# Forgetting attention with two products instead of three: high and low halves side by side in the array

## The reference

```
proj = u @ w_in                      # q, k, v, g (1024 columns each), fl (16 columns)
c = cumsum(log_sigmoid(fl + b_f))    # one value per row and head
for each head (16, of 64 columns), each block of 128 query rows:
    s = (qb @ k.T) * 0.125 + (cb[:, None] - c[None, :])      # causal, else -inf
    out = softmax(s) @ v
y = (out * silu(g)) @ w_out
```

## Time and profile before

| | |
|---|---|
| median of 3 runs | 3930.71 us (3926.98 to 3938.69) |
| profiled execution | 3930.58 us, span 3928.6 us |
| TensorE busy | 3640.7 us (93%) |
| VectorE busy | 2038.1 us (52%) |
| ScalarE busy | 1672.7 us (43%) |
| POOL busy | 108.0 us (3%) |
| mean granted TensorE clock | 0.951 |

### The profile page before, as it was taken

One profiled execution on the slowest core, in us unless ns is written; L12 is line 12 of the kernel. 1 busy time (PEld: TensorE's weight loads), 2 busy tenths in 40 slices (PEclk: granted clock), 3 DMA queues, 4 the chain that ended last, 5 costly groups with the idle time before them and its releaser, 6 DMA issues. The chain is left out here.

```text
span 3928.6 us, 48656 instructions
## 1 busy us (share of the span) xinstructions
PE 3640.7 (93%) x19058; PEld 2996.8 (76%) x19058; DVE 2038.1 (52%) x3959; ACT 1672.7 (43%) x3118; POOL 108.0 (3%) x119
## 2 busy tenths in 40 slices
PE   7999889999997999899897999999869999999799
PEld 6888558778876777777786877777758888888687
DVE  3144443453345677776335455555555456666552
ACT  3222561454442344443225444444443466665431
POOL 0011220000000000000000000000000000000000
PEclk9999999999997788989999999999979999999899
DMA  4343412113222211222311101010032121110321
GB/s 143 115 134 105 141 40 89 58 68 108 95 74 82 57 44 44 56 53 65 134 38 63 28 28 33 28 28 28 27 108 81 54 65 38 44 38 17 121 78 43
DMA packets 219339, 264.59 MB, mean 67 GB/s; under 512 B 62700, under 2 KB 142692, under 8 KB 218088
## 3 DMA queue, kind: packets, MB, share of 16 engines
q1 hardware_dynamic: 219112, 261.48, 20.6%
HBM read 191.43 MB, written 69.99 MB: 67 GB/s over the span
## 5 line engine op out<-in xcount | busy, mean ns | idle before, releaser
L332 PE MATMUL bank<-wh,XH 128*128 128x512 f32 x1344 | 536.3, 399 | 24.1 <-DVE wl L316 19.0
L332 PE MATMUL bank<-wh,XL 128*128 128x512 f32 x1344 | 529.1, 394 | 0.0
L332 PE MATMUL bank<-wl,XH 128*128 128x512 f32 x1344 | 528.5, 393 | 0.0
L2633 PE MATMUL bank<-XH,wh 128*128 128x512 f32 x1040 | 426.0, 410 | 28.2 <-DVE wl L2622 26.7
L2633 PE MATMUL bank<-XH,wl 128*128 128x512 f32 x1040 | 410.5, 395 | 0.0
L2633 PE MATMUL bank<-XL,wh 128*128 128x512 f32 x1040 | 409.6, 394 | 0.0
L332 PEld LDWEIGHTS bank<-wh,XH 128*128 128x128 f32 x1344 | 256.5, 191 | 77.9 <-DVE wl L316 12.6
L332 PEld LDWEIGHTS bank<-wl,XH 128*128 128x128 f32 x1344 | 255.8, 190 | 54.1
L332 PEld LDWEIGHTS bank<-wh,XL 128*128 128x128 f32 x1344 | 256.4, 191 | 51.0
L332 PE MATMUL bank<-XH,wh 128*128 128x512 f32 x704 | 280.8, 399 | 8.0 <-DVE XL L1585 8.0
L316 DVE TENSOR_TENSOR wl<-raw,wh 128x1024 fp32r<-128x1024 f32 x128 | 157.1, 1237 | 250.8 <-ACT wh L307 249.3
(11 more groups left out here) (419 smaller groups left out, 7155.0 us busy)
## 6 DMA issues: line engine op xcount, KB each, us to landing
sc_zt<-stage SPq DMA_DIRECT2D x88, 256.0 KB, 2.0
raw<-in_att_w_in SPq DMA_DIRECT2D x33, 512.0 KB, 4.1
raw<-in_even_w_in SPq DMA_DIRECT2D x32, 512.0 KB, 4.9
raw<-in_odd_w_in SPq DMA_DIRECT2D x32, 512.0 KB, 4.5
raw<-in_rec_w_in SPq DMA_DIRECT2D x32, 512.0 KB, 4.0
sc_h<-H SPq DMA_DIRECT2D x24, 512.0 KB, 2.6
sc_z<-stage SPq DMA_DIRECT2D x40, 256.0 KB, 2.0
z<-sc_z SPq DMA_DIRECT2D x8, 1024.0 KB, 5.8
```

The costliest lines, as they stand in the source:

```text
L332: done = e.matmul(out, lhsT, rhs, start=k == 0 and j == 0, stop=k == NK - 1 and j == 2)
L2633: done = e.matmul(bank[:, :], x[:, k, :], y[:, k, ts], start=k == 0 and j == 0, stop=k == NK - 1 and j == 2)
```

## The change

1. **Two products for scores.** The 64 rows beside the head's are now used. `qq` holds qh in the head's rows and ql in the other ones; `kk` holds kh in both. One product qq·kk gives high·high and low·high. The second, qx·kx, has qh and kl in the head's rows and the bias rows in the other ones. ScalarE makes two copies for each `load` instead of one.
2. **Two products for weighted.** v lies as [high, low] of one head (low, high for the other), so that one stationary operand gives vh·W in the head's 64 result rows and vl·W in the other 64. It meets WH, then WL. The two row halves must now be added: the new event `rest` copies the other rows from bank 5 to SBUF (ScalarE, 64x256), and `ve_mixed` adds them (64x256) and applies the gate in a second instruction that waits for the first.
3. **Gate.** Tanh of half the input instead of Sigmoid; plus one and times 0.5 are folded into the VectorE instructions.
4. **Order.** Low is done for n-2, behind the transposes of the same step and behind the maximum and scaling; `rest` and `mixed` are for n-5, in even steps; weight splits are at s = 2, 6, 10 and 14. Two events for n = 127 end the list.
5. **POOL.** The low halves of the seven blocks that come back are computed by POOL; buffers and later stages wait for its flag `xrest`.
6. The start-up fill clears two tiles for each head slot instead of four.

```diff
 def fox_order():
...
-        order += [("low", n - 3, 0)] * at(3) + [("turned", n - 2)] * at(2) + [("exps", n)] * at(0)
-        order += [("low", n - 3, 1)] * at(3) + [("normed", n - 1)] * at(1)
+        order += [("rest", n - 5)] * (at(5) and n % 2 == 0) + [("turned", n - 2)] * at(2) + [("exps", n)] * at(0)
+        order += [("normed", n - 1)] * at(1) + [("low", n - 2, half) for half in range(2)] * at(2)
+        order += [("mixed", n - 5)] * (at(5) and n % 2 == 0)
...
-            long |= {3: ("split", i + 1), 7: ("split", i + 2), 11: ("split", i + 3), 14: ("split", i + 4),
-                     8: ("load", 2 * p, "rows"), 9: ("load", 2 * p, "q"), 10: ("load", 2 * p, "k")}
...
+            long |= {8: ("load", 2 * p, "rows"), 9: ("load", 2 * p, "q"), 10: ("load", 2 * p, "k")}
...
+        if p < 8 and s % 4 == 2 and number[p, "q"] + s // 4 + 1 < len(seq):
+            order.append(("split", number[p, "q"] + s // 4 + 1))
...
+    order += [("rest", 127), ("mixed", 127)]
...
-            for j, (u, v) in enumerate((("qh", "kh"), ("ql", "kh"), ("qh", "kl"))):
+            for j, (u, v) in enumerate((("qq", "kk"), ("qx", "kx"))):
...
-            for j, (v, w) in enumerate(((vh, self.WH), (vl, self.WH), (vh, self.WL))):
-                done = e.matmul(bank[:, off:256], v[:, ks], w[x][:, kb, off:256], start=kb == top and j == 0,
-                                stop=kb == 0 and j == 2, skip_group_check=True)
+            off = P if kb == top else 0
+            for j, w in enumerate((self.WH, self.WL)):
+                done = e.matmul(bank[:, off:256], v[:, kb, :], w[x][:, kb, off:256], start=kb == top and j == 0,
+                                stop=kb == 0 and j == 1, skip_group_check=True)
...
+                scale, x, src = 0.125 if name == "q" else 1.0, self.x[n % 2], self.raw[name][hr, :]
+                e.activation(x[2 * name][hr, :], src, ACT.Copy, scale=scale).then_inc(*self.high.up("own", n, name))
+                second = x["qx"][hr, :] if name == "q" else x["kk"][self.other_rows(n), :]
+                e.activation(second, src, ACT.Copy, scale=scale).then_inc(*self.high.up(n, name))
...
+            if what == "rest":
+                h, x = n // 8, n // 2 % 2
+                e.wait_ge(*self.weighted.at(n))
+                if n >= 4:
+                    e.wait_ge(*self.mixed.at(n - 4))
+                e.activation(self.rest[x][self.rows_of(h)[0], :], c.banks[5][self.other_rows(h), 0:256], ACT.Copy).then_inc(*self.lower.up(n))
...
-            e.activation(self.half(self.g[p % 2], half), bank[:, :], ACT.Sigmoid).then_inc(*self.copied.up(p, name, half))
+            e.activation(self.half(self.g[p % 2], half), bank[:, :], ACT.Tanh, scale=0.5).then_inc(*self.copied.up(p, name, half))
...
+        e.wait_ge(*self.lower.at(n))
+        e.tensor_tensor(rest, self.c.banks[5][hr, 0:256], rest, ALU.add).then_inc(*self.mixed.up("sum", n))
+        e.wait_ge(*self.mixed.at("sum", n))
...
-        e.tensor_tensor(g, self.c.banks[5][hr, 0:256], g, ALU.mult).then_inc(*self.mixed.up(n))
+        e.scalar_tensor_tensor(out=g, in0=rest, scalar=0.5, in1=g, op0=ALU.mult, op1=ALU.mult).then_inc(*self.mixed.up(n))
...
+        for p in range(7):
+            e.wait_ge(*self.xhigh.at(p, 1))
+            e.tensor_tensor(self.c.XL[:, p, :], self.back_row(p), f32(self.c.XH[:, p, :]), ALU.subtract).then_inc(*self.xrest.up(p))
```

More of the change, by code:

```diff
@@ L2638 @@
 FOX_FIRST = ((0, "f", 0), (0, "q", 0))
-SPLITS = ("qh", "ql", "kh", "kl")
+SPLITS = ("qq", "kk", "qx", "kx")
 def fox_order():
@@ L2707, in __init__ @@
         self.tile = c.early("pe")
-        self.xlow = c.flag("ve")
+        self.xlow, self.xrest = c.flag("ve"), c.flag("po")
         self.w = HeadWeights(c, [win[:, 3984:4112]] + [win[:, at[name] + p * P:at[name] + (p + 1) * P] for p, name in self.seq[1:]],
-                             2, self.tile, [(self.xlow, (p, 1)) for p in range(7)])
+                             2, self.tile, [(self.xrest, (p,)) for p in range(7)])
         self.neg, self.negr, self.idr = c.const("neg"), c.sb("negr", [P, P], R32), c.sb("idr", [P, P], R32)
@@ L2732, in __init__ @@
         self.scored, self.turned, self.vturned, self.weighted = (c.flag("pe") for _ in range(4))
-        self.copied, self.high, self.expd, self.whigh, self.vhigh, self.xhigh, self.biased, self.logged = (c.flag("ac") for _ in range(8))
+        self.copied, self.high, self.expd, self.whigh, self.vhigh, self.xhigh, self.biased, self.logged, self.lower = (
+            c.flag("ac") for _ in range(9))
         self.ready, self.zeroed, self.low, self.most, self.scale, self.wlow, self.vlow, self.gated, self.mixed, self.summed = (
@@ L2736, in __init__ @@
         self.ones = c.flag("po")
-        self.marks = [[(self.xlow, (7, 123 + 4 * (s // 4)))] for s in range(NS)]
-        self.ends = [(self.xlow, (7, 127)), (self.ones, ())]
+        self.marks = [[(self.xrest, (6,))] * (s == 0) + [(self.xlow, (7, 123 + 4 * (s // 4)))] for s in range(NS)]
+        self.ends = [(self.xlow, (7, 127)), (self.xrest, (6,)), (self.ones, ())]
     def of(self, n):
@@ L2752, in rows_of, with other_rows, v_bank, v_high @@
         return slice(64 * (h % 2), 64 * (h % 2) + 64), 64 * (1 - h % 2)
+    def other_rows(self, h):
+        return slice(64 * (1 - h % 2), 64 * (1 - h % 2) + 64)
+    def v_bank(self, p, half):
+        return self.c.banks[self.mms[p, "v'", half]][:, :].rearrange("p (k a e) -> p k a e", k=4, a=2)
+    def v_high(self, p, half):
+        return self.v[p % 2][:, 4 * half:4 * half + 4, 0:4:3, :]
+    def v_low(self, p, half):
+        return self.v[p % 2][:, 4 * half:4 * half + 4, 1:3, :]
     def half(self, t, half):
@@ L2789, in sp @@
                 self.sp_rows(e, n)
-            elif what == "weighted" and n % 16 == 15 and n < 112:
+            elif what == "mixed" and n % 16 == 15 and n < 112:
                 p = n // 16
@@ L2952, in ac @@
                 e.activation(c.XH[:, n, :], self.back_row(n), ACT.Copy).then_inc(*self.xhigh.up(n, 1))
-            if what == "weighted" and n >= 112 and n % 4 == 3:
+            if what == "rest":
[4 more added lines that the diff above has]
+                e.activation(self.rest[x][self.rows_of(h)[0], :], c.banks[5][self.other_rows(h), 0:256], ACT.Copy).then_inc(*self.lower.up(n))
+            if what == "mixed" and n >= 112 and n % 4 == 3:
                 hr, half = self.rows_of(n // 8)[0], n % 8 // 4
@@ L3000, in ve @@
                 e.wait_ge(*self.copied.at(n, "g", rest[1]))
-                e.tensor_tensor(g, c.banks[self.mms[n, "g", rest[1]]][:, :], g, ALU.mult).then_inc(*self.gated.up(n, rest[1]))
+                e.scalar_tensor_tensor(out=g, in0=g, scalar=1.0, in1=c.banks[self.mms[n, "g", rest[1]]][:, :], op0=ALU.add, op1=ALU.mult) \
+                    .then_inc(*self.gated.up(n, rest[1]))
             elif what == "sums":
@@ L3029, in ve @@
                                     f32(self.WH[x][:, kbs[0]:kbs[-1] + 1, qs]), ALU.subtract).then_inc(*self.wlow.up(n, g))
[L3030 to L3034, removed]
+            elif what == "mixed":
+                self.ve_mixed(e, n)
     def ve_fill(self, e):
@@ L3043, in ve_fill @@
             other, at = slice(64 * (1 - hh), 64 * (1 - hh) + 64), 64 * (1 - hh)
-            for n in SPLITS:
+            for n in SPLITS[2:]:
                 done = e.tensor_copy(self.x[hh][n][other, :], self.e[0][other, :])
```

35 lines of the change are left out of this document (15 added, 20 removed).

## The result

The changed kernel takes 3786.47 us (median of 4 runs, 3782.67 to 3794.85) against 3928.85 for the kernel before, run beside it: a ratio of 0.9636, 95% interval 0.9613 to 0.966. The forecast was 3825 with a lower bound of 3797; the gain is 142.4 us where 105.9 were expected. The profiled execution took 3782.67 us, its span 3781.1, the mean granted clock 0.954.

A forecast was written before the change was run, and what follows sets the result against it. TensorE was taken to set the pace through seven pairs of heads, the chain between engines in the last; 3930.6 - 97.5 - 6 - 2.4 gave 3825 us, own range 3803 to 3850, overall range 3797 to 3866.

The forecast's parts named there:

- Products removed: Scores and weighted: dropping one product of three saves 8.7 us of TensorE a pair, 61 over seven.
- rival 5: TensorE's matmuls: no effect, because weight loads rather than columns set the pace; chance 0.02.
- Order: Seven pairs' steps: TensorE's waits for WL and wl, their restarts and slow matmuls go, 7.3 us a pair.
- Gate: Gate and exponential: all 28 table loads go with Tanh, freeing 0.9 us a pair of exponential waits and a restart.
- rival 2: Gate and exponential: table loads stay, costing 17 us over seven pairs, total 3842 us; chance 0.08.
- For these new meetings I keep 3.0 us a pair: Steps s = 1 and 2: ScalarE's added copies are tight there, so 3.0 us a pair allowed for new waits.
- rival 4: Weighted's bank hand-over through three engines: late `rest` stalls TensorE at 64 weighted, 2.0 us each gives 3953 us; chance 0.03.
- Rival 1: Seven pairs' steps: waits return for a late exponential or WH, all 8.2 us a pair, total 3861 us; chance 0.20.
- The last pair: Last pair of heads: minus 6 us in all, including 10 us for XL moved to POOL, bounds minus 25 and plus 14.
- Rival 3: Last pair: POOL and VectorE hold each other up, up to plus 14 us there, total 3845 us; chance 0.12.
- Start: Start of the stage: four fills of 0.61 us leave the chain, minus 2.4 us; bound 0.
- Sum: Whole kernel: 3930.6 us less 97.5 in the steps, 6 in the last pair and 2.4 at the start, 3825 us.

The follow-up runs named there:

- e2: The kernel before with only the order changed, keeping three products, Sigmoid and VectorE's subtraction: 3851.53 us, ratio 0.98; steps 575.3 us, last pair 78.2.
- e4: The changed kernel with the Sigmoid gate instead of Tanh, everything else kept: 3795.93 us, ratio 0.9663; steps 519.0 us.
- e1: The changed kernel put back to the old order and Sigmoid, with two products kept: 3961.51 us, ratio 1.0079; steps 663.2 us.
- e5: The changed kernel with `rest` and the gate back right behind weighted: 3828.42 us, ratio 0.9739; steps 544.3 us.
- e6: The changed kernel with the low halves back to n-3, around the maximum: 3846.83 us, ratio 0.9786; steps 559.9 us.
- e7: The changed kernel with the weight splits back at s = 3, 7, 11 and 14: 3821.69 us, ratio 0.973; steps 549.9 us.
- e8: The changed kernel with the returning rows' low halves on VectorE instead of POOL: 3791.2 us, ratio 0.9647; last pair 81.4 us.
- e12: The changed kernel with the first three returning loads issued early and low halves on VectorE: 3783.64 us, ratio 0.9628; last pair 75.9 us.
- e9: The changed kernel with the first three returning loads issued ahead of SyncE's wait for `mixed` 111: 3785.17 us, ratio 0.9633; last pair 75.8 us.
- e10: The changed kernel with each POOL subtraction of 128x1024 issued as four of 128x256: 3785.48 us, ratio 0.9633; last pair 75.1 us.

## Why the prediction came out too high

**Products removed: right.** With the new order in place, two products instead of three take 56.3 us off the steps (e2 to e4, which also moves the gate to n-5), 60.0 off TensorE's busy time; the sum had 61 (8.7 a pair). So rival 5 falls.

**Order: right in kind, a little small.** Alone it gives 58.5 us (633.8 to 575.3), 8.4 a pair where 7.3 (51.1 in seven) stood. TensorE's idle time falls by 40.5 us and its busy time for the same matmuls by 17.9. The first was put at 4.6 a pair, 32; the second, restarts and the slow stretch, at 2.7 a pair, 19. That the second came so near is partly luck: I had counted six slow matmuls of 512 columns in every pair, and the kernel before has 22 in all seven.

**Gate: right in kind, a little small.** Tanh takes 10.2 us off (519.0 to 508.8), 1.5 a pair where 0.9 (6.3 in seven) stood. Of the table loads of the gate and the exponential this one is left, ahead of the steps:

```profile
L2996 ACT ACT_TABLE_LOAD x1 | 1.3, 1283 | 0.0
```

So Tanh and Exp do alternate without a load, and rival 2 falls. ScalarE is busy 38.4 us less than in e4 and the steps are 10.2 us shorter: most of a table load's 1.28 us lay beside TensorE's work. The Trainium skill's rule ("ScalarE: Activation LUTs", section "Table sets: the hidden batching unit"), that tanh lies in the exponential's set, agrees with this row.

**"For these new meetings I keep 3.0 us a pair": this is the step that failed.** It put 21 us of new waits into the seven pairs. There are none: TensorE is idle 1.4 us in 508.8. A pair takes 72.7 us, that is the 70.7 of matmuls and the 2.0 of small change at transposes; of the 1.0 that I had left standing, mostly for the v copy, and of the 3.0 nothing is there. The reason for the 3.0 was that ScalarE's copies at s = 1 and 2 are about as long as TensorE's two steps. In the changed kernel two such steps of a middle pair, 9.10 us, look like this:

```profile
2408.00:2417.10 9.10, 9.10 (x54) 7.89 (x53) 5.49 (x9) 6.76 (x11) 0.00 (x0) 1.00 0.00 0
```

ScalarE is busy 6.76 us, less than I had reckoned, and TensorE all of the 9.10. And the argument asks only whether the engine is busy, not when its results are wanted. ScalarE's and VectorE's groups show `rest` and the addition at their new places:

```profile
L2976 ACT ACTIVATE rest<-bank 64x256 f32<-64x256 f32 x64 | 24.3, 380 | 8.3 <-PE bank L2908 6.8
...
L3121 DVE TENSOR_TENSOR rest<-bank,rest 64x256 f32<-64x256 f32 x64 | 26.7, 417 | 4.2 <-ACT rest L2976 3.3
```

VectorE idles 4.2 us before its 64 additions, the last pair's included, where in e1's steps it idled 158.6 before 54, and before the gate in the kernel before 176.6. I had read those 176.6 us as slack against rival 4. They were also time in which VectorE, in order, held back the low halves behind the gate. The kernel before shows it itself, in its timelines of VectorE and TensorE: 4.51 us at the gate, then a split, then the WL for which TensorE stands.

```profile
2468.99 0.43 DVE L3100 TENSOR_TENSOR gg<-bank,gg 64x256 f32<-64x256 f32 x1 [4.51 <-PE bank L2891]
2469.34 1.22 DVE L3014 SCALAR_TENSOR_TENSOR ql<-rawq,qh 64x1024 fp32r<-64x1024 f32 x1
2470.58 0.69 DVE L3027 TENSOR_TENSOR WL<-bank,WH 128x512 fp32r<-128x512 f32 x1
```
```profile
2471.42 0.30 PE L2854 MATMUL bank<-ident,w 128*128 128x128 f32 x1 [0.44 <-DVE WL L3027]
```

The change lets the gate stand until its operand is there. With `rest` and the gate back at the old place, 35.5 us of the steps' gain are gone (e5): the new place leaves the room that the 3.0 us did not reckon with.

**Products and order do not add up.** My sum took them as independent; this holds only in the order in which the change has both. Two products give -56.3 us in the new order and +29.4 in the old one (663.2 against 633.8). Rival 1, waits come back, and the hand-over of rival 4 are real in e1: 40.2 us of TensorE's busy time go, 70 us of idle time come. They do not occur in the changed kernel, where `rest`, low halves and splits stand otherwise (e5 to e7).

**The last pair: right sign, too small.** It is 16.9 us shorter, not 6. The order alone gives that (e2: 78.2, with three products and VectorE's subtraction); I had not counted the order there at all. POOL's part is 3.3 us (e8 against after) or 0.1 (e12 against e9), not 10, and the first load is indeed later, 6.60 us of wait for 3.50, as I had it. Rival 3 is shown as a mechanism: about 6.7 us of stretched VectorE instructions beside seven POOL ones of 2.35 to 2.88 us. But what it costs is at most what it frees, so it did not decide. The Trainium skill ("SBUF — State Buffer", section "Who interferes with whom") has the rule that such instructions exclude each other for a whole instruction; the pair of rows at 2721.12 and 2720.70 agrees. The seven of VectorE's reductions from PSUM that ran beside POOL were not stretched (0.41 to 0.68 us, as without it).

**Start: wrong by 2.4.** The four fills went from the chain, but ScalarE's second half of the first tile then waited for TensorE instead, as its timeline shows, and the first maximum came no earlier:

```profile
2132.55 0.68 ACT L3001 ACTIVATE w<-bank,fb 32x512 f32<-32x512 f32 x1 [2.18 <-PE bank L2633]
```

**Sum.** Steps -125.0 for -97.5, 27.5 more: 21.0 for the new meetings, 7.4 for the order, 3.9 for the gate, less 4.6 for the products; the 0.2 left over is rounding. The last pair is 10.9 off, the start 2.4 the other way. Of the median's difference to the forecast, 38.5 us, about 36 are accounted for so; the rest lies within what the unchanged part moves.

**Open.** That the late load, the meetings and the clock are the whole of what limits the last pair was not shown. Why two products make it 3.2 us longer where VectorE does the subtraction (e8 against e2) was not tried; e8's first load is waited for 6.08 us there, e2's 3.33, and the granted clock is 0.77 against 0.87.

## What to carry to other kernels

On in-order engines, first ask for every event at which step its operand is ready and at which its result is wanted, and let it stand between the two; only then compare busy times. A saving of matmuls that adds a hand-over can turn into a loss in the old order and be worth its full price in a new one, so try the two together before judging either. Work given to POOL beside VectorE on the path is worth trying in pieces, and here a wait removed in front of such a meeting paid in full only once the meeting was short too.

## What the runs showed of the hardware

A VectorE instruction of 0.16 us took 1.96 us, and one of 0.29 took 2.30, beside a POOL subtraction of 128x1024, and ended within 0.1 us of POOL's instruction. In e10, with POOL's work in 128x256 pieces of 0.78 us, the same two forms took at most 0.50 and 0.69 us, and the longest, a scaling of 128x1024, 1.25 instead of 0.75; POOL itself was busy longer, 20.9 us instead of 17.1.

And the same 2,870 or so matmuls kept TensorE busy 507.4 us with 1.4 us of waits, at a granted clock of 1.00, and 547.6 us with 115.7 us of waits among them, at 0.95: in that pair of kernels each microsecond of wait came with a third of a microsecond of longer matmuls. The same work can also begin at another clock by chance: the first ten us of the last pair ran at 0.99 in the changed kernel and at 0.83 in e10.
